# Sums and broadcasts of two norms: from quarters of TensorE's array to the whole array

## The reference

```python
def l2norm(t):
    return t * lax.rsqrt(jnp.sum(t * t, axis=-1, keepdims=True) + EPS)

qb = l2norm(heads(qb, GDN_HEADS)) * GDN_HEAD_DIM ** -0.5    # first norm: 4 heads of q
kb = l2norm(heads(kb, GDN_HEADS))                           # and 4 heads of k
...
o_a = rmsnorm(o_a, hg_norm_w) * sigmoid(...)                # second norm: outputs of the
o_b = rmsnorm(o_b, gdn_norm_w) * silu(...)                  # 4 + 4 heads
```

## Time and profile before

| | |
|---|---|
| median of 3 runs | 1088.95 us (1087.48 to 1090.53) |
| the profiled execution, its own time | 1088.95 us |
| its span, first to last instruction | 1086.8 us |
| mean granted clock of TensorE | 0.995 |
| busy: PE, DVE, ACT, POOL | 97%, 63%, 47%, 7% |

### The profile page before, as it was taken

The page is one execution under the profiler, slowest core; times in us unless marked ns, Lnnn a source line. Parts: engine busy times, 40 slices in busy tenths (PEclk is TensorE's granted clock), DMA queues, the critical chain, the costliest instruction groups (busy, mean ns, idle before and its releaser), DMA issues.

```text
span 1086.8 us, 21480 instructions
## 1 busy us (share of the span) xinstructions
PE 1050.6 (97%) x8449; PEld 1029.5 (95%) x8449; DVE 679.4 (63%) x873; ACT 510.8 (47%) x681; POOL 77.9 (7%) x144
## 2 busy tenths in 40 slices
PE   6999999998999998999999999999999999999998
PEld 5999999987899997999999999999999989999997
DVE  5766654567876656776665457666644986666543
ACT  5444443454773443654444346444433654444334
POOL 8100000020000110200000011000000120000001
PEclk9999999999999999999999999999999999999999
DMA  6656655897695421566665558666565437566551
GB/s 199 195 175 175 187 174 180 134 230 134 129 127 143 140 74 44 158 195 185 179 176 178 188 156 237 184 178 176 172 195 174 136 104 210 175 176 187 178 175 40
DMA packets 135061, 177.91 MB, mean 164 GB/s; under 512 B 5806, under 2 KB 120574, under 8 KB 134992
## 3 DMA queue, kind: packets, MB, share of 16 engines
q1 hardware_dynamic: 131616, 165.78, 54.8%
q0 software_dynamic: 3328, 11.38, 3.7%
q10 hardware_dynamic: 64, 0.02, 0.0%
HBM read 171.19 MB, written 6.52 MB: 164 GB/s over the span
## 4 chain that ended last, share of the span: by engine, by line
PE 86%; DVE 7%; ACT 4%; issue 2%; DMA 0%; ACTq 0%; SPq 0%; DVEq 0%
PE ps L1491 26%; PE ps L1492 25%; PE ps L1493 25%; PE ps L1317 1%; ACT w_hi L511 1%; DVE C L618 1%; PE ps L1324 1%; DVE w_lo L1020 1%; PE ps L1306 1%; DVE xw_lo L1041 1%; DVE x L1029 1%; PE ps L1287 1%; PE ps L1336 1%; PE ps L1606 1%; PE ps L1517 1%
## 5 line engine op out<-in xcount | busy, mean ns | idle before, releaser
L1020 DVE TENSOR_TENSOR w_lo<-raw,w_hi 128x1024 fp32r<-128x1024 f32 x312 | 381.6, 1226 | 305.1 <-ACT w_hi L511 303.6
L511 ACT CAST w_hi<-raw 128x1024 fp32r<-128x1024 f32 x312 | 325.6, 1049 | 454.6 <-PE ps L1493 429.7
L1491 PE MATMUL ps<-xw_hi,w_hi 128*128 128x264 f32 x1472 | 421.2, 286 | 2.2 <-issue 1.0
L1492 PE MATMUL ps<-xw_lo,w_hi 128*128 128x264 f32 x1472 | 420.2, 285 | 0.0
L1493 PE MATMUL ps<-xw_hi,w_lo 128*128 128x264 f32 x1472 | 419.3, 285 | 0.0
L1491 PEld LDWEIGHTS ps<-xw_hi,w_hi 128*128 128x128 f32 x1472 | 278.2, 189 | 5.0 <-issue 3.9
L1493 PEld LDWEIGHTS ps<-xw_hi,w_lo 128*128 128x128 f32 x1472 | 277.5, 189 | 0.0
L1492 PEld LDWEIGHTS ps<-xw_lo,w_hi 128*128 128x128 f32 x1472 | 277.2, 188 | 0.1
L1493 PE MATMUL ps<-a_hi,w_lo 128*128 (+1 forms) x704 | 200.4, 285 | 0.0
L1491 PE MATMUL ps<-a_hi,w_hi 128*128 (+1 forms) x704 | 200.1, 284 | 0.0
L1492 PE MATMUL ps<-a_lo,w_hi 128*128 (+1 forms) x704 | 200.0, 284 | 0.0
(11 more groups left out here) (335 smaller groups left out, 798.1 us busy)
## 6 DMA issues: line engine op xcount, KB each, us to landing
raw<-in_ffn_w_gate SPq DMA_DIRECT2D x88, 512.0 KB, 3.8
raw<-in_ffn_w_up SPq DMA_DIRECT2D x88, 512.0 KB, 3.8
raw<-in_ffn_w_down SPq DMA_DIRECT2D x88, 512.0 KB, 3.4
raw<-in_w_in_even SPq DMA_DIRECT2D x32, 512.0 KB, 7.9
raw<-in_w_out_even SPq DMA_DIRECT2D x8, 512.0 KB, 5.0
raw<-in_pool_w_in SPq DMA_DIRECT2D x8, 512.0 KB, 3.5
out<-SBUFS POOLq DMA_DIRECT2D x4, 512.0 KB, 3.9
PT<-in_x_prompt SPq DMA_DIRECT2D x2, 512.0 KB
```

Source lines behind the costliest of these rows:

```text
L511: nc.scalar.copy(w_hi[:, w % SPL, :], raw[:, w % RAW, :]).then_inc(hi_done, 1)
L1020: nc.vector.tensor_tensor(w_lo[:, w % SPL, :], raw[:, w % RAW, :], w_hi[:, w % SPL, :].bitcast(F32), ALU.subtract).then_inc(lo_done, 1)
L1491: mm(out, wh, hi, start=first, stop=False)
L1492: mm(out, wh, lo, start=False, stop=False)
```

## The change

All matmuls of both norms use the whole array. The sums of the first norm go into 8 rows of one bank: for head d the weights are a 128x8 tile whose column d is one (`esel`), and the 8 matmuls accumulate. The sums of the second norm go into 4 rows in the same way with 1/128 in the column (`emean`), so the root has no scale. The broadcasts take a column of the identity over 128 rows and all 128 rows of `RN` or `RN2`, which POOL fills with zeros at the start, so that rows 8 to 127 hold zeros. Root, reciprocal and scale work on 8 or 4 partitions. POOL builds `qscale` with one affine_select, has no wait on `consts` of its own, and fills `esel` and `emean` with two fills and 16 of one column each.

```diff
-        part_sel = sb("part_sel", [P, 48])
-        qscale = sb("qscale", [P, 1])
+        esel = sb("esel", [P, 8, 8])
+        emean = sb("emean", [P, 8, 8])
+        qscale = sb("qscale", [8, 1])
...
-            A.activation(RN[:, :], ps[:, 7, 0:TOK], ACT.Sqrt, bias=eps[:, 0:1])
+            A.activation(RN[0:8, :], ps[0:8, 7, 0:TOK], ACT.Sqrt, bias=eps[0:8, 0:1])
...
-            A.activation(RN[:, :], ps[:, 0, 0:TOK], ACT.Sqrt, bias=eps[:, 0:1], scale=1.0 / DH)
+            A.activation(RN[0:4, :], ps[0:4, 0, 0:TOK], ACT.Sqrt, bias=eps[0:4, 0:1])
...
-            A.activation(RN2[:, :], ps[:, 6, 0:TOK], ACT.Sqrt, bias=eps[:, 0:1], scale=1.0 / DH)
+            A.activation(RN2[0:4, :], ps[0:4, 6, 0:TOK], ACT.Sqrt, bias=eps[0:4, 0:1])
...
-            link(V.reciprocal(RN[:, :], RN[:, :]))
-            V.tensor_scalar(RN[:, :], RN[:, :], qscale[:, 0:1], None, ALU.mult)
+            link(V.reciprocal(RN[0:8, :], RN[0:8, :]))
+            V.tensor_scalar(RN[0:8, :], RN[0:8, :], qscale[:, 0:1], None, ALU.mult)
...
-                f = (RN, RN2)[y][:, :]
+                f = RN2[0:4, :] if y else RN[0:4, :]
...
-            for y in range(2):
-                for h in range(4):
-                    ins = mm(ps[32 * h:32 * h + 32, 7, 0:TOK], part_sel[:, 16 - 16 * y:48 - 16 * y], hn[:, 4 * y + h, :],
-                             start=y == 0, stop=y == 1)
+            for d in range(8):
+                ins = mm(ps[0:8, 7, 0:TOK], esel[:, d, :], hn[:, d, :], start=d == 0, stop=d == 7)
...
-                    rows, one = slice(32 * h, 32 * h + 32), 32 * h + 4 * t0
-                    ins = mm(ps[:, 4 + h, 0:TOK], ident[rows, one:one + 1].broadcast_to([32, P]), RN[rows, :],
+                    ins = mm(ps[:, 4 + h, 0:TOK], ident[:, t0 + h:t0 + h + 1].broadcast_to([P, P]), RN[:, :],
                              start=True, stop=True)
...
-                for h in range(4):
-                    ins = mm(ps[32 * h:32 * h + 32, bank, 0:TOK], ones[:, 0:32], hn[:, 4 * y + h, :], start=True,
-                             stop=True)
+                for d in range(4):
+                    ins = mm(ps[0:4, bank, 0:TOK], emean[:, d, 0:4], hn[:, 4 * y + d, :], start=d == 0, stop=d == 3)
...
-                    rows = slice(32 * h, 32 * h + 32)
-                    ins = mm(ps[:, 4 * y + h, 0:TOK], ident[rows, 32 * h:32 * h + 1].broadcast_to([32, P]), f[rows, :],
-                             start=True, stop=True)
+                    ins = mm(ps[:, 4 * y + h, 0:TOK], ident[:, h:h + 1].broadcast_to([P, P]), f, start=True,
+                             stop=True)
...
-            for h in range(4):
-                ins = G.memset(qscale[32 * h:32 * h + 16, :], DH ** -0.5)
...
-            pool.wait_ge(st("consts"), 2)
+            G.affine_select(out=qscale[:, :], in_=qscale[:, :], compare_op=ALU.is_ge, fill=DH ** -0.5, base=-4,
+                            pattern=[[0, 1]], channel_multiplier=1).then_inc(st("consts"), 1)
...
+            link(G.memset(RN[:, :], 0.0))
+            link(G.memset(RN2[:, :], 0.0))
...
-            link(G.memset(part_sel[:, :], 0.0))
-            G.memset(part_sel[:, 16:32], 1.0).then_inc(st("consts"), 1)
-            pool.wait_ge(st("consts"), 4)
+            link(G.memset(esel[:, :, :], 0.0))
+            link(G.memset(emean[:, :, :], 0.0))
+            for d in range(8):
+                G.memset(esel[:, d, d:d + 1], 1.0)
+                ins = G.memset(emean[:, d, d:d + 1], 1.0 / DH)
+            ins.then_inc(st("consts"), 1)
```

More of the change, by code:

```diff
@@ L372, in even_scalar @@
             act.wait_ge(st("norm_ss"), 1)
-            A.activation(RN[:, :], ps[:, 7, 0:TOK], ACT.Sqrt, bias=eps[:, 0:1]).then_inc(st("norm_root"), 1)
+            A.activation(RN[0:8, :], ps[0:8, 7, 0:TOK], ACT.Sqrt, bias=eps[0:8, 0:1]).then_inc(st("norm_root"), 1)
             slots(18, 22)
@@ L460, in even_scalar @@
             act.wait_ge(st("qk_n"), 2)
-            A.activation(RN[:, :], ps[:, 0, 0:TOK], ACT.Sqrt, bias=eps[:, 0:1], scale=1.0 / DH).then_inc(st("norm_root"), 1)
+            A.activation(RN[0:4, :], ps[0:4, 0, 0:TOK], ACT.Sqrt, bias=eps[0:4, 0:1]).then_inc(st("norm_root"), 1)
             act.wait_ge(st("o_mm"), 1)
@@ L467, in even_scalar @@
             act.wait_ge(st("norm_ss"), 3)
-            A.activation(RN2[:, :], ps[:, 6, 0:TOK], ACT.Sqrt, bias=eps[:, 0:1], scale=1.0 / DH).then_inc(st("norm_root"), 1)
+            A.activation(RN2[0:4, :], ps[0:4, 6, 0:TOK], ACT.Sqrt, bias=eps[0:4, 0:1]).then_inc(st("norm_root"), 1)
             samples_stored(act, (4, 5))
@@ L713, in even_vector @@
             dve.wait_ge(st("norm_root"), 1)
-            link(V.reciprocal(RN[:, :], RN[:, :]))
-            V.tensor_scalar(RN[:, :], RN[:, :], qscale[:, 0:1], None, ALU.mult).then_inc(st("norm_r"), 1)
+            link(V.reciprocal(RN[0:8, :], RN[0:8, :]))
+            V.tensor_scalar(RN[0:8, :], RN[0:8, :], qscale[:, 0:1], None, ALU.mult).then_inc(st("norm_r"), 1)
             slots(18, 20)
@@ L1691, in _ @@
             link(G.memset(qscale[:, :], 1.0))
-            for h in range(4):
-                ins = G.memset(qscale[32 * h:32 * h + 16, :], DH ** -0.5)
-                if h < 3:
-                    link(ins)
-            ins.then_inc(st("consts"), 1)
-            pool.wait_ge(st("consts"), 2)
+            G.affine_select(out=qscale[:, :], in_=qscale[:, :], compare_op=ALU.is_ge, fill=DH ** -0.5, base=-4,
+                            pattern=[[0, 1]], channel_multiplier=1).then_inc(st("consts"), 1)
             link(G.memset(SEL[:, :, :], 1.0))
```

## The result

Six runs of the changed kernel have a median of 1095.21 us (1093.80 to 1096.49), six of the kernel before, beside them, 1088.80 us (1086.67 to 1090.53). The ratio is 1.0061, 95% interval 1.0048 to 1.0076: +6.6 us, between +5.2 and +8.3.

The account below looks back on a forecast made before the run. TensorE was taken to bound the kernel (86% of the chain), except where it waits for others, as for VectorE around the first norm. Onto 1088.95 us came 4.0 + 2.2 = +6.2 us, giving 1095.2 us, range 1092.0 to 1098.5.

Parts of the forecast that it names:

- first stretch: First norm, 288.71 to 307.04 us: gross 4.84 us less waits of 0.43 and 0.39 us, net +4.0 us.
- The sum of 8: First norm's sum of squares, 8 matmuls: from 1.03 to 3.65 us, +2.62 us, priced from L1189.
- The sum of 4: Second norm's sums of squares, 4 matmuls each: 1.89 us; the first delays L1415 by 1.04 us.
- The broadcast: Four matmuls, both norms: from 0.65 to 1.76 us, +1.11 us each; +1.20 us for an engine waiting for the result.
- Both waits for VectorE: TensorE's first-norm waits, 0.43 us for the evacuation and 0.39 us for L725, both claimed to go.
- Second stretch: Second norm, 418.07 to 436 us: +2.2 us with output projection's first slot at full clock, +3.4 at half clock.
- Main case: Output projection's first slot at full clock: 4.0 + 2.2 = +6.2 us, 1095.2 us; chance 0.52.
- first rival: Half clock at the output projection: 4.0 + 3.4 = +7.4 us, 1096.4 us; chance 0.22.
- The clock's near cases: TensorE idle 1.93 us ahead of 288.71, clock stayed; 2.04 ahead of 266.26, clock fell; first taken for the output projection.
- The fills: GpSimd's 18 more fills delay the state loads by up to 5.4 us, under 78 us of cover; price nothing.
- Absorbed later: Waits at the mixer's levels (346 to 408 us) take in the first 4.0 us; +2.2, 1091.2 us; chance 0.14.
- Nothing absorbed: Both VectorE waits stay and the second sum of squares is paid: gross 9.2 us, 1098.2 us; chance 0.12.

Follow-up runs that it names:

- changed with sum early: Changed kernel with the first norm's sum moved to bank 6 and behind VectorE's L705, so it fills TensorE's idle time; 1.0035, +3.8 us against the kernel before.
- second norm alone: Kernel before with the change made in the second norm only; ratio 1.0029, +3.2 us.
- sum twice: Changed kernel with the first norm's sum of 8 matmuls done twice in a row, same result; ratio 1.0086, +9.4 us against the kernel before.
- the sums alone: Kernel before with only the sums of squares over the whole array, broadcasts left on quarters; ratio 1.0020, +2.2 us.
- first norm alone: Kernel before with the change made in the first norm only; ratio 1.0037, +4.0 us.
- fills alone: Kernel before plus GpSimd's new fills (RN, RN2, esel, emean) and nothing else; ratio 0.9995, -0.5 us.
- before with the sum early: Kernel before with the first norm's sum in bank 6 and behind VectorE's L704 instead of ScalarE's copy; ratio 1.0008, +0.9 us.
- the last kernel: Kernel before with second norm's first broadcast moved ahead of the state matmuls, unread matmuls ahead of the output projection and of input-projection slots 8 and 12; 0.9993, -0.8 us.
- both kernels with quarters and an early sum: Kernel before with the early sum, 1.0008; and that plus second norm's first broadcast moved ahead of the state matmuls and three unread matmuls, 0.9989.

## Why the prediction came out

**Direction and size.** 1095.2 forecast, 1095.21 measured. The mechanism was right. That the two agree to the hundredth is luck: the first stretch was set 0.4 us too long, the second at the lower of two values that both occur, and the runs of a kernel lie 1.5 us to either side of their median.

**Prices of the groups.** The sum of 8: 3.65 forecast, 3.66 found. The sum of 4: 1.89 forecast, 422.53 - 420.65 = 1.88 found. The broadcast: 1.76 forecast from L1479, 1.59 found from start to start. Records do start 0.22 us apart, but the next matmul's first record begins earlier and lasts longer (0.48 instead of 0.39 us); with the slot behind it, it is 4.70 us against 4.80 reckoned. The 2.0 us that stand beside the 1.76 as an estimate are a quarter above what was found.

**First stretch: +4.0 forecast, +3.64 found.** Both waits for VectorE vanished as reckoned, shown by the changed kernel's missing brackets, by its chain, and by the kernel with the sum done twice, which paid all of it. Of the missing 0.4 us, 0.2 is the two broadcasts, and 0.2 the slots 17 to 19: 291.31 to 300.21 is 8.90 us where three times 3.04 was set. The slot's length was the mis-sized term: 3.04 was read from the one slot behind the second broadcast, and the three in a row took 2.97 each.

**Second stretch: +2.2 or +3.4 forecast, +2.20 and +3.33 found.** L925 came 2.11 us later after the first broadcast (2.24 reckoned) and 2.20 after the second. The second sum was hidden, the reciprocal held up the second broadcast by 0.18 us (0.2 reckoned). Main case and first rival were not alternatives, though: of four profiles with the second norm changed, two kept the clock (changed, changed with sum early) and two lost it (second norm alone, sum twice). If the clock falls in half of the executions, the mean of both, +2.8, and 3.6 of the first stretch make 6.4 us, which is what the medians differ by; that share was not measured. By it, the forecast's 6.2 had 0.4 too much in the first stretch and 0.6 too little in the second.

**The clock's near cases.** The prediction took two waits of the kernel before as near cases, the clock kept behind 1.93 us and lost behind 2.04. It had a third one, 2.23 us ahead of 251.22, behind which the clock stayed at 1.00. So the cases did not speak for either value, and the main case's 0.52 against 0.22 had less behind it than it seemed.

**What costs nothing.** The fills: 221.09 instead of 220.82 for the state loads, 0.27 us later where the bound was 5.4, and no time in the kernel that has only them. Fewer rows save nothing either: root 0.47 us, reciprocal 1.79, against 0.48 and 1.80 over 128.

**The rivals.** Absorbed later: out. The distance between the stretches is 110.92 to 111.04 us in all fourteen profiles, whatever the first stretch had lost or gained, and behind the second one the changed kernel is only 0.4 us shorter. Nothing absorbed: out for the sums alone (+2.2 where it said +4.5) and, by the profiles, for the whole change (3.64 and 2.20, or 3.33 with the clock down, instead of 9.2). The rival's sum put 1.11 us on the second sum of squares, which costs 1.24 by the prediction's own prices; nothing hangs on that. The clock of the kernel before at the projection had been taken as fallen, and it had in all four profiles whose second norm was that of before (before, first norm alone, fills alone, before with the sum early).

## What to carry to other kernels

Matmuls that need only a quarter of the array's rows or columns are worth putting side by side; undoing that costs what the timeline gives for the same forms elsewhere in the kernel, less the waits on the same engine in the same stretch. Look for those waits before summing: here they took 1.2 of 4.8 us in one stretch, slots shorter than reckoned included, and a whole group in the other. And an engine's idle time is only worth filling where that engine sets the stretch: the same move won 1.9 to 2.5 us of the stretch in one kernel and moved a wait in the other.

## What the runs showed of the hardware

TensorE's granted clock fell from 1.00 to 0.50 behind single waits of 1.9 to 3.2 us, and stayed up behind others of the same length. Over the fourteen profiles, one of each kernel:

- Ahead of slot 8 of the input projection TensorE waited 2.2 to 2.9 us in thirteen of them. In six (the changed kernel among them) the clock fell there; in these the wait ahead of slot 12 was 1.5 us, and it stayed up behind that. In the other seven (the kernel before among them) it stayed up at slot 8, the wait ahead of slot 12 was 2.0 to 2.1 us, and it fell behind that: one of the two falls in every profile, never both. The fourteenth has both waits filled up with unread matmuls to 0.9 and 0.7 us, and fell at neither.
- Ahead of the sum of the first norm, where it was not moved, TensorE waited 1.9 us in the profiles with the fall at slot 12 and 2.4 to 2.5 in those with the fall at slot 8, and the clock stayed up in all ten. In the one profile with neither fall it waited 2.58 us and the clock fell.
- Ahead of the output projection the clock fell behind 2.43 or 2.44 us in four of four and behind 3.20 in the one case; behind 1.91 or 1.92 us it fell in two of four; behind waits of 1.43 us or less it stayed up in all five.

What a fall costs depends on who sets the stretch: nothing at slot 8, 1.0 us at slot 12 (22.45 us from there to the sum in the kernel before, 21.42 in the changed one), 1.1 to 1.3 us (21.47 - 20.34, 18.07 to 18.26 - 16.96) at the output projection in most profiles, and 2.3 us there (19.27 - 16.96) in the one where slot 0 took 5.55 us.

Filling one idle stretch was followed by a fall at another one: in the last kernel at the sum, and in both kernels with quarters and an early sum at slot 18, where the wait grew to 2.29 and 2.59 us. That the filling brought it about is not shown; it would take several profiles of one kernel.
